# The last weight slot's part for the second half of the row: one accumulating bank against two separate banks of 256 columns

## What is computed

```
for i in range(DEPTH):                    # first block: stages 0 to 3
    y = windowed_gqa(h, ...)              # or recurrent_block(h, ...)
    x = layer_norm(DN_ALPHA * x + (1.0 + gate) * y, ln_g[i, 0], ln_b[i, 0])
    y = sq_relu_mlp(x * (1.0 + scale) + shift, mlp_w1[i], mlp_w2[i])
    x = layer_norm(DN_ALPHA * x + (1.0 + gate) * y, ln_g[i, 1], ln_b[i, 1])
for i in range(DEPTH):                    # second block: stages 4 to 9
    x = layernorm(DN_ALPHA_2 * x + 0.5 * swiglu(x, w13, w2), ...)
    x = layernorm(DN_ALPHA_2 * x + hybrid_mixer(x, ...), ...)
    x = layernorm(DN_ALPHA_2 * x + 0.5 * swiglu(x, w13, w2), ...)
def layer_norm(x, g, b):
    mu = jnp.mean(xf, axis=-1, keepdims=True)
    var = jnp.mean(jnp.square(xf - mu), axis=-1, keepdims=True)
    y = (xf - mu) * lax.rsqrt(var + LN_EPS)
```

## Time and profile before

| | |
|---|---|
| median of 3 runs | 2277.94 us (2277.34 to 2278.91) |
| profiled execution | 2276.05 us, of which the span from first to last instruction is 2274.2 us |
| TensorE matmul busy | 2177.2 us, 96% of the span |
| VectorE busy | 1570.1 us, 69% |
| ScalarE busy | 1132.9 us, 50% |
| granted TensorE clock, mean | 0.987 of full speed |
| DMA | 396.95 MB, mean 175 GB/s |
| chain of waits that ended last | PE 73%, DVE 16%, ACT 5%, issue 3%, DMA 1% |

### The profile page before, as it was taken

How to read it: one execution, slowest core, us unless ns; L and a number is a source line. 1 busy time by engine, 2 the same in 40 slices (tenths; PEclk the granted TensorE clock), 3 DMA queues, 4 the chain that set the end, 5 groups by cost and what they waited for, 6 DMA issues and landing times.

```text
span 2274.2 us, 36179 instructions
## 1 busy us (share of the span) xinstructions
PE 2177.2 (96%) x15272; PEld 2004.2 (88%) x15272; DVE 1570.1 (69%) x1888; ACT 1132.9 (50%) x1516; POOL 326.8 (14%) x273
## 2 busy tenths in 40 slices
PE   4889999998999999999999999999999999999998
PEld 4779898887899899998899899999999988998997
DVE  6879987798755754569865674465456996757445
ACT  3344434786544443456664453444345766445332
POOL 2112324111110210030010130012003000212000
PEclk9899999998999999999999999999999999999999
DMA  9749894344465455665432455546566554235552
GB/s 359 237 149 326 312 334 142 109 113 118 136 209 192 158 201 187 166 189 149 121 116 71 148 193 185 182 150 220 185 183 168 156 132 112 94 114 186 195 191 93
DMA packets 304053, 396.95 MB, mean 175 GB/s; under 512 B 47103, under 2 KB 262777, under 8 KB 303892
## 3 DMA queue, kind: packets, MB, share of 16 engines
q1 hardware_dynamic: 285440, 336.75, 46.2%
q0 software_dynamic: 17472, 57.57, 8.1%
q10 hardware_dynamic: 980, 0.32, 0.1%
HBM read 393.53 MB, written 1.07 MB: 174 GB/s over the span
## 4 chain that ended last, share of the span: by engine, by line
PE 73%; DVE 16%; ACT 5%; issue 3%; DMA 1%; POOL 0%; SPq 0%; DVEq 0%; ACTq 0%; POOLq 0%
PE tiles L523 15%; PE tiles L524 15%; PE tiles L525 15%; PE y_rows L523 6%; PE y_rows L524 6%; PE y_rows L525 6%; DVE weights_lo L1437 4%; PE tiles L934 2%; ACT weights_hi L1052 2%; DVE ada_acc L1487 2%; DMA ada_ring<-in_ada_w_dram 1%; DVE rnn_r L1771 1%; ACT xt L1089 1%; DVE rnn_conv_out L1737 1%; PE tiles L654 1%
## 5 line engine op out<-in xcount | busy, mean ns | idle before, releaser
L1437 DVE TENSOR_TENSOR weights_lo<-weights_raw,weights_hi 128x2048 fp32r<-128x2048 f32 (+2 forms) x316 | 767.8, 2438 | 431.7 <-ACT weights_hi L1052 431.0
L523 PE MATMUL tiles<-xt_hi,weights_hi 128*128 128x256 f32 (+1 forms) x3200 | 912.9, 285 | 13.7 <-ACT xt L1089 7.0
L524 PE MATMUL tiles<-xt_lo,weights_hi 128*128 128x256 f32 (+1 forms) x3200 | 906.8, 283 | 0.0
L525 PE MATMUL tiles<-xt_hi,weights_lo 128*128 128x256 f32 (+1 forms) x3200 | 906.6, 283 | 0.0
L1052 ACT ACTIVATE weights_hi<-weights_raw 128x2048 fp32r<-128x2048 f32 (+2 forms) x316 | 592.3, 1878 | 217.5 <-PE y_rows L525 168.7
L523 PEld LDWEIGHTS tiles<-xt_hi,weights_hi 128*128 128x128 f32 (+1 forms) x3200 | 608.1, 190 | 29.0 <-issue 22.5
L524 PEld LDWEIGHTS tiles<-xt_lo,weights_hi 128*128 128x128 f32 (+1 forms) x3200 | 608.3, 190 | 2.8
L525 PEld LDWEIGHTS tiles<-xt_hi,weights_lo 128*128 128x128 f32 (+1 forms) x3200 | 608.2, 190 | 0.0
L523 PE MATMUL y_rows<-weights_hi,hid_hi 128*128 128x512 f32 x608 | 239.4, 394 | 0.8 <-DVE weights_lo L1437 0.8
L524 PE MATMUL y_rows<-weights_lo,hid_hi 128*128 128x512 f32 x608 | 237.8, 391 | 0.0
L525 PE MATMUL y_rows<-weights_hi,hid_lo 128*128 128x512 f32 x608 | 237.1, 390 | 0.0
(11 more groups left out here) (367 smaller groups left out, 2737.5 us busy)
## 6 DMA issues: line engine op xcount, KB each, us to landing
weights_raw<-in_ffn_w_dram SPq DMA_DIRECT2D x132, 1024.0 KB, 5.0
weights_raw<-in_mlp_w_dram SPq DMA_DIRECT2D x64, 1024.0 KB, 5.7
weights_raw<-in_w_in_dram SPq DMA_DIRECT2D x52, 1024.0 KB, 5.3
ada_ring<-in_ada_w_dram POOLq DMA_DIRECT2D x76, 512.0 KB, 5.3
weights_raw<-in_rnn_w_in_dram SPq DMA_DIRECT2D x16, 768.0 KB, 4.6
weights_raw<-in_w_in_dram SPq DMA_DIRECT2D x32, 256.0 KB, 4.3
weights_raw<-in_w_branch_a_dram SPq DMA_DIRECT2D x32, 256.0 KB, 4.8
weights_raw<-in_w_branch_b_dram SPq DMA_DIRECT2D x8, 1024.0 KB, 5.3
```

What stands on the lines that cost most here:

```text
L523: pe.matmul(o, a, c, start=first, stop=False)
L524: pe.matmul(o, a, d, start=False, stop=False)
L525: return pe.matmul(o, b, c, start=False, stop=last)
L1437: dve.tensor_tensor(slot_view(WLO, m, NSPL), slot_view(RAW, m, NRAW), slot_view(WHI, m, NSPL).bitcast(F32), ALU.subtract).then_inc(*inc("l ...
```

## The change

In `rows_tail`, slot a's part for the second half of tile 1 now closes the accumulation in `Y` and reports `rows_done`. Slot b's part for these 512 columns no longer adds to it: it goes in two pieces of 256 columns into two banks that `topen` takes from the ring (`("yq", s, 0)` and `("yq", s, 1)`), six matmuls each. In `norm`, VectorE takes the second half's residual from `Y` once slot a's part is done, then adds each piece's bank to the rows, with the gate through `XS` in stages 0 to 3 and in one instruction in stages 4 to 9, and takes statistics of each 256 columns by themselves. The aggregate of tile 1 reads three groups of statistics; `ln_stats` has room for them and stands elsewhere. Whoever waited for slot b's `rows_done` now waits for the second piece, and ScalarE's write of the next gate rows waits until VectorE is through with it.

```diff
--- before.py
+++ after.py
@@ -171,10 +171,11 @@
         SNK = put("sinks1", [P, 8])
         SNK2 = put("sinks2", [P, 2, 16])
         AL2 = put("a_log_dt", [8, 8])
-        ST = put("ln_stats", [P, NT, 2, 6])
         MV = put("ln_mean_var", [P, NT, 2])
         RV = put("ln_rstd", [P, NT, 4])
         RCOL = put("rnn_decay_cols", [RB_W, 8, 32])
+        pos["at"] += 96
+        ST = put("ln_stats", [P, NT, 3, 6], at=pos["at"])
         AT1 = put("attn_small", [P, 6, 16])
         A2S = put("attn2_small", [P, 3, 8])
         GCOL = put("g_cols", [P, 6, 8])
@@ -398,7 +399,11 @@
             total[n % NRAW] += 16 * len(x[3])
             landed_at[n] = total[n % NRAW]
 
-        y_end = {x[0][0]: ("rows_done", x[0]) for x in slots if x[0][1] in ("w2", "out")}
+        y_end = {x[0][0]: x[0] for x in slots if x[0][1] in ("w2", "out")}
+        for s, label in y_end.items():
+            slot_end[number[label]] = ("tile_done", ("yq", s, 1))
+
+        y_before = {s: (s, x[1], x[2] - 1) for s, x in y_end.items()}
 
         def slot_view(ring, n, depth):
             _, p, (a_, b_), _ = slots[n]
@@ -582,10 +587,17 @@
                 ins.then_inc(*inc("y_half", s))
                 rows_part(*a, False, False, 1, 0)
                 rows_part(*b, False, True, 1, 0).then_inc(*inc("y_third", s))
-                rows_part(*a, False, False, 1, 1).then_inc(*inc("rows_done", la))
+                rows_part(*a, False, True, 1, 1).then_inc(*inc("rows_done", la))
                 if s + 1 < n_sub:
                     prep(s + 1, 0)
-                rows_part(*b, False, True, 1, 1).then_inc(*inc("rows_done", lb))
+                n, wh, wl = open_slot(lb)
+                for q in range(2):
+                    bank = topen(("yq", s, q), "D")
+                    w = slice(512 + q * S, 512 + (q + 1) * S)
+                    for kk in range(2):
+                        xa, xb = b[1](b[3] + kk)[:, P:S], b[2](b[3] + kk)[:, P:S]
+                        ins = mm3(bank[:, 0:S], xa, xb, wh[:, kk, w], wl[:, kk, w], kk == 0, kk == 1)
+                    ins.then_inc(*inc("tile_done", ("yq", s, q)))
                 if s + 1 < n_sub:
                     keep_busy(s, b, WARM_ROWS)
                     prep(s + 1, 1)
@@ -1078,7 +1090,7 @@
                 for h in range(2):
                     bank = tile(("gate", s, h))
                     if s > 0 and h == 0:
-                        act.wait_ge(*past("y_free", (s - 1, 1)))
+                        act.wait_ge(*past("free_D", ("yq", s - 1, 1)))
                     evac(("gate", s, h), GATE[:, h * 512:(h + 1) * 512], src=bank)
 
             def modulate(s, t, g, k0, k1):
@@ -1618,7 +1630,7 @@
 
             def variance(s, t):
 
-                dve.bn_aggr(MV[:, t, :], ST[:, t, :, :].rearrange("p a b -> p (a b)")).then_inc(*inc("ln_var", (s, t)))
+                dve.bn_aggr(MV[:, t, :], ST[:, t, 0:2 + t, :].rearrange("p a b -> p (a b)")).then_inc(*inc("ln_var", (s, t)))
 
             def scale_rows(s, t):
 
@@ -1650,10 +1662,23 @@
                 dve.wait_ge(*past("y_third", s))
                 residual(s, 1, 0, 512)
                 dve.bn_stats(ST[:, 1, 0, :], XN[:, 1, 0:512]).then_inc(*inc("ln_part", s))
-                dve.wait_ge(*past(*y_end[s]))
+                dve.wait_ge(*past("rows_done", y_before[s]))
                 residual(s, 1, 512, D)
+                for q in range(2):
+                    w = slice(512 + q * S, 512 + (q + 1) * S)
+                    bank = tile(("yq", s, q))[:, 0:S]
+                    x = XN[:, 1, w]
+                    if s < 4:
+                        t = XS[:, 1, w]
+                        dve.tensor_tensor(t, bank, GATE[:, w], ALU.mult).then_inc(*inc("free_D", ("yq", s, q)))
+                        dve.wait_ge(*past("free_D", ("yq", s, q)))
+                        chain(dve.tensor_tensor(x, x, t, ALU.add))
+                    else:
+                        dve.scalar_tensor_tensor(x, bank, 1.0 if is_mix(s) else 0.5, x, ALU.mult, ALU.add).then_inc(*inc("free_D", ("yq", s, q)))
+                        dve.wait_ge(*past("free_D", ("yq", s, q)))
+                    ins = dve.bn_stats(ST[:, 1, 1 + q, :], x)
                 dve.wait_ge(*past("ln_part", s))
-                chain(dve.bn_stats(ST[:, 1, 1, :], XN[:, 1, 512:D]))
+                chain(ins)
                 variance(s, 1)
                 scale_rows(s, 1)
                 if s + 1 < n_sub:
```

## The result

The changed kernel takes 2286.24 us (median of 6 runs, 2284.72 to 2287.30) against 2276.98 (6 runs, 2275.33 to 2278.91): a ratio of 1.0041, with a 95% interval from 1.0030 to 1.0052, so +9.3 us with an interval from 6.8 to 11.8. The forecast was slower, 2289.0, in a range from 2283 to 2296. Its profiled execution took 2284.72 us, with a span of 2282.9.

A forecast was written before the change was run, and what follows sets the result against it. TensorE, busy 96% of the span, was taken to bound the kernel, with VectorE late at the ends of stages 1 to 3. Profiled 2276.05 + 7.45 (VectorE) + 3.6 (clock) = 2287.1, on the median 2289.0 us; range 2283 to 2296.

The forecast's parts named there:

- What bounds the boundary: Ends of stages 1 to 3: VectorE, not TensorE, is late, without slack; stages 4 to 8 have 0.81 us.
- TensorE's part: Twelve matmuls of 256 columns replace six of 512: 0.06 us more per boundary, hidden everywhere by the gap before the transposes.
- VectorE's part: Added VectorE instructions delay tile 1's aggregate at the ten boundaries, 7.45 us in all; bounds 3.3 and 12.9.
- Rule against rows: VectorE's instruction spacing: trace rows (0.61 us unwaited, 0.727 waited) preferred to the Trainium skill's rule, which would give 7.9 us.
- The clock: Longer TensorE gaps, 2.6 us, at the ends of stages 1 to 3 lower the clock: three falls of 1.2 us, 3.6 us.
- The sum: Whole kernel: profiled 2276.05 + 7.45 + 3.6 = 2287.1 us, put on the median of the runs as 2289.0.
- Cheap pieces: Rival: VectorE's statistics of 256 columns cost near 0.21 us and the clock holds; 2281.2 us, chance 0.07.
- TensorE last: Rival: TensorE's last matmul ends last at each boundary, so pieces gain 6.6 us; 2271.3 us, chance 0.04.
- The clock holds: Rival: no clock fall behind the longer gaps, only VectorE's added work remains; 2285.4 us, chance 0.22.
- a low stretch twice as long: Rival: low clock behind stages 1 to 3 lasts twice as long, costing 3 x 3.0 = 9 us; 2294.4 us, chance 0.10.

The follow-up runs named there:

- gated_only: The change made only at the ends of stages 0 to 3, the old form elsewhere: 2286.01 us, ratio 1.0040 to the kernel before.
- ungated_only: The change made only at the ends of stages 4 to 8, the old form elsewhere: 2277.47 us, ratio 1.0004 to the kernel before.
- act_scale: Kernel before, stages 0 to 3: slot b's part ahead of tile 0's transposes, tile 0's scaling moved to ScalarE, 28 unused matmuls; 2272.50 us, ratio 0.9982.
- b_first: Kernel before, slot b's last part moved ahead of tile 0's transposes in stages 0 to 3, 34 unused matmuls for 22; 2274.47 us, ratio 0.9993.
- te_pieces: Kernel before with slot b's last part as twelve matmuls of 256 columns into the same bank, VectorE unchanged; 2277.13 us, ratio 1.0003.
- after_filled: Changed kernel with 36 instead of 22 unused matmuls filling TensorE's gap in stages 0 to 3; 2283.71 us, ratio 1.0030 to the kernel before.
- before_gap: Kernel before with 8 instead of 22 unused matmuls in stages 0 to 3, widening TensorE's gap; 2279.41 us, ratio 1.0015.
- one_bank: Changed kernel with one bank and one piece of 512 columns instead of two of 256; 2284.34 us, ratio 1.0034 to the kernel before.
- late_new: Kernel before plus 16 unused matmuls ahead of slot b's last part and the change, both in stages 4 to 8; 2285.30 us (2285.72 without the change).

## Why the prediction was right, point by point

- **What bounds the boundary.** Right, and shown from both sides: gated_only has the loss, ungated_only hardly any, act_scale gains 0.84 of the 0.9 us it takes off VectorE at each boundary, b_first gains mostly where VectorE waited.
- **TensorE's part, 0.06 us.** Right in size (te_pieces). That it is hidden everywhere was wrong: it is paid at 0.04 to 0.06 in each of stages 1 to 8, some 0.4 us in te_pieces. In the changed kernel, where VectorE never waits for it, it is hidden.
- **VectorE's part, 7.45 us.** The traces show 8.0. Stages 1 to 3 were put at +1.71 and are +1.77 to +1.79, stage 0 at +0.92 and is +1.00, stages 4 to 8 at +0.08 and are +0.13, stage 9 at +1.00 and is +1.04. Statistics of 256 columns were taken at 0.42 and are 0.427. The 0.05 to 0.08 missing at each is for the most part the second wait ahead of the aggregate (0.06), which I had counted as one. The aggregate of 18 numbers takes 0.24 against 0.21 us; that 0.03 lies behind the start that the table reads, and comes on top.
- **Rule against rows.** The changed kernel's rows agree with those of before: 0.61 us without a wait (366.86 to 367.47), 0.73 with one (368.17 to 368.90). The prediction has these rows against the Trainium skill ("VectorE: DVE Perf Modes", The DRAIN you can't avoid) in both cases. Only one of them holds. That section of the Trainium skill says that a semaphore costs nothing extra. The trace disagrees, 0.73 against 0.61. But the same section of the Trainium skill also says that a next instruction that is not held starts earlier, which the prediction left out. The trace agrees, 0.61 after the start of one that takes 0.69.
- **The clock, 3.6 us.** That a gap of this size can bring the low clock was right; where it falls and what one fall costs weren't. I forecast a fall behind each of stages 1 to 3 and none behind stage 0. The profiled execution had one behind stage 2 and one behind stage 0, because stage 0's gap was 2.7 us too: its slot b ran at the full clock this time and the 22 unused matmuls ended early. In gated_only slot b ran at the low clock, the gap was 1.22 us and no fall followed, which is the case that the prediction had counted. The fall behind stage 2 cost 0.63 us and not 1.2; what the one behind stage 0 cost can't be told apart from the rest of stage 1. In the medians the term is 2.0 to 2.5 us (after_filled, not told from none) or 2.9 us (before_gap, 1.4 to 5.5 by its interval). The falls that the traces price don't add up to that, so the size of this term stays open.
- **The sum.** 8.0 and 2.5 make 10.5, the measured difference is 9.3 with an interval from 6.8 to 11.8; the forecast of 11.05 lies in it, near its upper end. Part of that is luck: VectorE's part was put 0.55 too low and the clock's about 1 us too high. The range doesn't test the clock's term either, since 8.0 alone on the median of 2276.98 is 2285.0 and lies in it. In the profiled executions it closes: 8.0 at the boundaries and +0.6 over all the stages' own work make 8.6 of the 8.7 us between the spans. That 0.6 is a balance: +0.5 ahead of stage 0's first aggregate, +0.63 behind stage 2 and +1.1 in stage 8's own work, where a low stretch fell at 1965.3 and none in the kernel before, against -0.8 and -0.9 in stages 1 and 2. In stage 2 the kernel before had four low stretches, three of them of 6.8 us, and the changed one three of 3.4. That need not be chance: gated_only and one_bank have three there too, and all the other kernels four. Why is open.
- **The rivals.** Cheap pieces is refuted (0.427). TensorE last holds nowhere in this kernel; late_new makes it true and shows the sign that it named, and that its price was too high, since it counted only what follows the last piece. The clock holds was true at two of the four gaps, and a low stretch twice as long occurred in before_gap.

## What to carry to other kernels

Cutting the last piece of work finer shortens what follows it, but only the consumer's idle time pays for the added instructions. Most of them came here not from the cut but from the separate banks, which need one more pass over the rows (1.34 of 1.78 us in stage 1). So read the consumer's idle time just ahead of that piece, stage by stage, before cutting. Here it was nothing in stages 1 to 3 and 9, and the change added 1.0 to 1.8 us there; it was 0.81 in stages 4 to 8, and the change added 0.13. Where the consumer is late, take work off it (act_scale); bringing the producer's part forward gained 0.17 us a boundary there (b_first). And compare boundary by boundary in the traces: an effect of 0.1 us can be read there that no median of whole executions shows.

## What I had not expected of the hardware

The same gap of TensorE was followed by a lower clock at one boundary and not at another: 2.64 us behind stages 1, 2 and 3 of before_gap gave 0.50, 0.50 for twice as long, and 1.00. With 1.0 us none followed in any profiled execution. Two waits in a row on VectorE cost 0.10 us over the instruction ahead of them, one 0.04.
